# Seven products of half-size blocks in place of eight, in sixteen of 22 units of each up phase, with the inner tensor kept whole

## The reference, cut to what matters

```
def swiglu_ffn(x, w_in, w_out):              # twice: "up0/down0", "up1/down1"
    gate, up = jnp.split(x @ w_in, 2, axis=-1)
    return (jax.nn.silu(gate) * up) @ w_out
...
def conv_ffn(x, w_up, conv_w, conv_b, w_down):   # twice: "up2/down2", "up3/down3"
    up = x @ w_up
    a, g = up[..., :D_FF_2], up[..., D_FF_2:]
    g = causal_dwconv(g, conv_w) + conv_b        # three taps along the tokens
    return (jax.nn.gelu(g) * a) @ w_down
```

## Time and profile before

| | us |
|---|---|
| median of 3 runs | 2401.2 (2400.77 to 2401.31) |
| the profiled execution | 2402.46 |
| its span from first to last instruction | 2400.6 |
| TensorE busy | 2385.5 |
| VectorE busy | 1094.6 |
| ScalarE busy | 806.7 |
| GpSimd busy | 65.3 |
| mean granted TensorE clock | 0.998 of 2.4 GHz |

### The profile page before, as it was taken

One profiled execution on the slowest core, in us unless ns is written; L12 is line 12 of the kernel. 1 busy time (PEld: TensorE's weight loads), 2 busy tenths in 40 slices (PEclk: granted clock), 3 DMA queues, 4 the chain that ended last, 5 costly groups with the idle time before them and its releaser, 6 DMA issues.

```text
span 2400.6 us, 27033 instructions
## 1 busy us (share of the span) xinstructions
PE 2385.5 (99%) x12158; PEld 2026.4 (84%) x12158; DVE 1094.6 (46%) x1040; ACT 806.7 (34%) x891; POOL 65.3 (3%) x39
## 2 busy tenths in 40 slices
PE   9999999999999999999999999999999999999998
PEld 8888889898788888898987888888888977888887
DVE  4333225574553332256735544424545546544424
ACT  4222225455542222233432433322322432333311
POOL 0000000230100000000000000000000000000000
PEclk9999999999999999999999999999999999999999
DMA  4223323212132223142521222231432511222321
GB/s 163 103 91 105 106 88 126 76 37 88 39 120 90 104 90 112 70 164 87 177 73 56 103 101 95 98 115 66 153 106 72 191 70 71 88 105 88 122 90 68
DMA packets 34691, 238.30 MB, mean 99 GB/s; under 512 B 4108, under 2 KB 4492, under 8 KB 6800
## 3 DMA queue, kind: packets, MB, share of 16 engines
q1 hardware_dynamic: 34432, 236.56, 27.7%
q10 hardware_dynamic: 144, 0.00, 0.0%
HBM read 234.46 MB, written 2.10 MB: 99 GB/s over the span
## 4 chain that ended last, share of the span: by engine, by line
PE 98%; DVE 1%; ACT 1%; issue 0%; DMA 0%; DVEq 0%
PE bank L452 55%; PE bank L526 28%; PE bank L491 4%; PE bank L873 4%; PE bank L514 1%; PE bank L900 1%; PE bank L727 1%; PE bank L920 1%; PE bank L659 0%; PE bank L669 0%; PE bank L567 0%; DVE xn L1545 0%; PE bank L628 0%; PE bank L911 0%; PE bank L654 0%
## 5 line engine op out<-in xcount | busy, mean ns | idle before, releaser
L452 PE MATMUL bank<-a_hi,w_hi 128*128 128x512 f32 (+1 forms) x2112 | 787.2, 373 | 0.4 <-DVE a_lo L1590 0.4
L452 PE MATMUL bank<-a_hi,w_lo 128*128 128x512 f32 (+1 forms) x2112 | 782.8, 371 | 0.0
L452 PE MATMUL bank<-a_lo,w_hi 128*128 128x512 f32 (+1 forms) x2112 | 782.8, 371 | 0.0
L1520 DVE TENSOR_TENSOR w_lo<-raw,w_hi 128x2048 fp32r<-128x2048 f32 x207 | 476.5, 2302 | 502.3 <-ACT w_hi L1043 501.8
L1043 ACT ACTIVATE w_hi<-raw 128x2048 fp32r<-128x2048 f32 x207 | 394.5, 1906 | 357.2 <-DMA raw<-w_full 357.2
L452 PEld LDWEIGHTS bank<-a_hi,w_hi 128*128 128x128 f32 x2112 | 398.8, 189 | 69.9 <-issue 1.7
L452 PEld LDWEIGHTS bank<-a_hi,w_lo 128*128 128x128 f32 x2112 | 398.7, 189 | 67.7 <-issue 0.7
L452 PEld LDWEIGHTS bank<-a_lo,w_hi 128*128 128x128 f32 x2112 | 398.6, 189 | 67.1
L526 PE MATMUL bank<-w_hi,h_hi 128*128 128x512 f32 x692 | 270.1, 390 | 0.0
L526 PE MATMUL bank<-w_hi,h_lo 128*128 128x512 f32 x692 | 269.6, 390 | 0.0
L526 PE MATMUL bank<-w_lo,h_hi 128*128 128x512 f32 x692 | 269.6, 390 | 0.0
(11 more groups left out here) (297 smaller groups left out, 2320.1 us busy)
## 6 DMA issues: line engine op xcount, KB each, us to landing
raw<-w_full SPq DMA_DIRECT2D x207, 1024.0 KB, 4.8
rows_ab<-rows SPq DMA_DIRECT2D x8, 1024.0 KB, 5.4
x<-x SPq DMA_DIRECT2D x4, 512.0 KB, 6.4
mem_raw<-mem SPq DMA_DIRECT2D x2, 1024.0 KB, 8.2
out<-x SPq DMA_DIRECT2D x3, 512.0 KB, 2.6
raw<-w_full SPq DMA_DIRECT2D x2, 512.0 KB, 6.3
ab_rows<-ab_rows SPq DMA_DIRECT2D x1, 768.0 KB, 7.6
wg_raw<-w_gates SPq DMA_DIRECT2D x1, 512.0 KB, 5.8
```

The costliest lines, as they stand in the source:

```text
L452: last = mm(bank[:, b + m, cols], w[:, s, c0:c0 + P], act_in[:, k, cols], start=(k == 0 and j == 0), stop=(k == KD - 1 and j == 2))
L1520: V.tensor_tensor(w_lo[:, u % SLOTS, :], raw[:, u % SLOTS, :], w_hi[:, u % SLOTS, :], ALU.subtract).then_inc(w_split, 1)
```

## The change

Units 4 to 19 of each up phase (`SEVEN0`, `SEVEN1`), 64 in all, are computed as a 2x2 by 2x2 block product with seven products (the form with shared sums): the two row blocks are the gate's 128 columns and the other half's 128 columns of the unit, the inner dimension is halved to 4 tiles, and the tokens are halved to 256.

- **TensorE** (`seven_unit`): 7 products of 12 matmuls of 256 columns, into four banks, in place of 48 of 512 columns. Two products use `a_hi`/`a_lo` and the weights as they are; the others use sums of weights (`s23`, `s4`, and one in place in `raw`), sums of tokens (`t`), or both.
- **GpSimd** (`up`): at the start of an up phase, behind the split of the last tokens, four sums of token blocks, ten operations of 128x1024. For each of the 16 units four sums of 128x512: one in place in `raw` before ScalarE's copy, and three behind the sixth product of unit u - 2.
- **ScalarE**: high parts of the sums (128x1024 and 128x512 per unit), a copy of the first product out of PSUM, on which the unit's last product waits. The high part of the inner tensor moves to the down phase.
- **VectorE** (`seven_results`): five additions from PSUM that recombine the products into `gate_c` and `h32`; the taps and the multiply then read SBUF on both inputs. Low parts of the sums. The low part of the inner tensor moves to the down phase.
- The inner tensor is kept whole as `h32` (44 KB per partition) and split in four stages of two blocks (`hidden_high`, `hidden_low`) in the last two units of the up phase and in the down phase. The down phase takes tokens in order 0 to 3.
- Some semaphores are merged (`small_in`), and the gain rows are loaded behind unit 19 of the up phase.

The core of the diff:

```
+SEVEN0, SEVEN1 = 4, 20
...
+            def add_up(dst, terms):
+                (first, _), (second, op) = terms[:2]
+                ins = G.tensor_tensor(dst, first, second, op)
+                for term, op in terms[2:]:
+                    link(ins)
+                    ins = G.tensor_tensor(dst, dst, term, op)
+                return ins
...
+            def first_weight_sum(f, u):
+                g = U0[f"up{f}"] + u
+                w = raw[:, g % SLOTS, :]
+                gp.wait_ge(w_loaded[g % SLOTS], 16 * (g // SLOTS + 1))
+                G.tensor_tensor(w[:, 2 * QS:3 * QS], w[:, 2 * QS:3 * QS], w[:, 3 * QS:4 * QS],
+                                ALU.add).then_inc(first_sum, 1)
...
+                gp.wait_ge(first_sum, j + 1)
+                if u >= SEVEN0 + 2:
+                    gp.wait_ge(gemm_done, gemm_at(f"up{f}", u - 2, 0))
+                link(G.tensor_tensor(s2, w[:, 2 * QS:3 * QS], w[:, 0:QS], ALU.subtract))
+                G.tensor_tensor(s3, w[:, 3 * QS:4 * QS], s2, ALU.subtract)
+                G.tensor_tensor(s4, w[:, QS:2 * QS], s2, ALU.subtract).then_inc(rest_sums, 1)
+
+            def up(f):
+                gp.wait_ge(a_lo_tok, TURN0[UP_GEN[f]] + NT)
+                token_sums(f, 1)
+                token_sums(f, 3)
+                first_weight_sum(f, SEVEN0)
+                rest_weight_sums(f, SEVEN0)
+                token_sums(f, 2)
+                token_sums(f, 4)
+                first_weight_sum(f, SEVEN0 + 1)
...
+                pe.wait_ge(w_split, U0[name] + u + 1)
+                bank_wait(name, u)
+                product(b, 0, w, 0, b_block(0, 0)).then_inc(first_product, 1)
+                product(b + 1, 0, w, QS, b_block(1, 0))
+                pe.wait_ge(t_split, 4 * f + 2)
+                product(b + 2, 1, w, 2 * QS, t_block(1))
+                pe.wait_ge(s_split, j + 1)
+                product(b + 2, 0, s23, QS, t_block(3))
+                product(b + 3, 1, s4, 0, b_block(1, 1))
+                pe.wait_ge(t_split, 4 * f + 4)
+                product(b + 1, 1, s23, 0, t_block(2)).then_inc(gemm_done, 1)
+                pe.wait_ge(first_copied, j + 1)
+                product(b, 1, w, 3 * QS, t_block(4)).then_inc(gemm_done, 1)
...
+            def copy_first(f, u):
+                act.wait_ge(first_product, nth_seven(f, u) + 1)
+                S.activation(h32[:, u, 0:256], bank[:, up_bank(u), 0:256], ACT.Copy).then_inc(first_copied, 1)
+
+            def hidden_high(f, u):
+                act.wait_ge(*hidden_at(f, 2 * u + 1))
+                act.wait_ge(*stage_free(f, u))
+                S.activation(h_hi[:, stage(u), :], h32[:, 2 * u:2 * u + 2, :], ACT.Copy).then_inc(h_high, 1)
...
+            def low_sums(f, u):
+                j = nth_seven(f, u)
+                dve.wait_ge(s_high, j + 1)
+                V.tensor_tensor(s23_lo[:, j % 2, :], s23_raw[:, j % 2, :], s23_hi[:, j % 2, :], ALU.subtract)
+                V.tensor_tensor(s4_lo[:, j % 2, :], s4_raw[:, j % 2, :], s4_hi[:, j % 2, :],
+                                ALU.subtract).then_inc(s_split, 1)
...
+                    if is_seven(n + 2) and n + 2 > SEVEN0:
+                        split_upto(U0[name] + n + 2)
                     dve.wait_ge(gate_done, F0[f] + n + 1)
-                    dve.wait_ge(gemm_done, gemm_at(name, n))
-                    V.tensor_tensor(h32[:, s, :], act_out[:, s, :], bank[:, b + 1, :], ALU.mult).then_inc(ffn_banks, 1)
-                    dve.wait_ge(h_hi_done, F0[f] + n + 1)
-                    V.tensor_tensor(h_lo[:, n, :], h32[:, s, :], h_hi[:, n, :], ALU.subtract).then_inc(h_done, 1)
-                    split_upto(U0[name] + n + 3)
+                    if is_seven(n):
+                        dve.wait_ge(ffn_banks, F0[f] + n + 1)
+                        V.tensor_tensor(h32[:, n, :], gate_s[:, s, :], h32[:, n, :], ALU.mult).then_inc(h_done, 1)
```

More of the change, by code:

```diff
@@ new lines, in up @@
+            def up(f):
[7 more added lines that the diff above has]
+                first_weight_sum(f, SEVEN0 + 1)
+                for u in range(SEVEN0 + 1, SEVEN1):
+                    rest_weight_sums(f, u)
+                    if u + 1 < SEVEN1:
+                        first_weight_sum(f, u + 1)
@@ L461, in feature_units, with seven_unit, product, b_block @@
                         feature_tile(name, u, m, slice(0, T)).then_inc(gemm_done, 1)
+            def seven_unit(f, u):
+                name = f"up{f}"
+                j, s, b = nth_seven(f, u), (U0[name] + u) % SLOTS, up_bank(u)
+                w, acts = (w_hi[:, s, :], w_lo[:, s, :]), (a_hi, a_lo)
+                s23 = s23_hi[:, j % 2, :], s23_lo[:, j % 2, :]
+                s4 = s4_hi[:, j % 2, :], s4_lo[:, j % 2, :]
+                def product(dst, half, weights, c0, moving):
+                    (hi, lo), (m_high, m_low) = weights, moving
+                    for k in range(KD // 2):
+                        for i, (st, mv) in enumerate(((hi, m_high), (lo, m_high), (hi, m_low))):
+                            last = mm(bank[:, dst, 256 * half:256 * half + 256], st[:, c0 + k * P:c0 + k * P + P], mv[:, k, :],
+                                      start=(k == 0 and i == 0), stop=(k == KD // 2 - 1 and i == 2))
+                    return last
+                def b_block(k, n):
+                    return block_b(a_hi, k, n), block_b(a_lo, k, n)
+                def t_block(n):
+                    return t_hi[:, n - 1, :, :], t_lo[:, n - 1, :, :]
+                pe.wait_ge(w_split, U0[name] + u + 1)
[11 more added lines that the diff above has]
+                product(b, 1, w, 3 * QS, t_block(4)).then_inc(gemm_done, 1)
@@ L1001, in _ @@
             head_units("up0", "start")
-            feature_units("up0", 2, KF)
+            up_units(0)
             down("down0", 0)
@@ L1005, in _ @@
             head_units("up1", "mixout")
-            feature_units("up1", 2, KF)
+            up_units(1)
             down("down1", 1)
@@ new lines, in up, with down_parts @@
+                    if is_seven(n + 1):
+                        copy_first(f, n + 1)
+                    if n + 3 < SEVEN0:
+                        split_upto(U0[name] + n + 3)
+                    elif n + 2 >= SEVEN1:
+                        split_upto(U0[name] + n + 2 + max(0, min(n - SEVEN1 + 1, 1)))
+                    if n >= SEVEN1:
+                        hidden_high(f, n - SEVEN1)
+            def down_parts(f):
+                name = f"down{f}"
+                for u in range(KF - SEVEN1, UNITS[name]):
+                    hidden_high(f, u)
+                    split_upto(U0[name] + u + 1)
@@ L1615, in rms_out, with down_parts @@
+                    if n >= SEVEN1:
+                        hidden_low(f, n - SEVEN1)
+            def down_parts(f):
+                name = f"down{f}"
+                for u in range(KF - SEVEN1, UNITS[name]):
+                    hidden_low(f, u)
+                    split_upto(U0[name] + u + 1)
             def rms_out(name, again):
                 end = U0[name] + UNITS[name]
-                split_upto(end)
+                down_parts(int(name[-1]))
                 rows_ready(name)
```

256 lines of the change are left out of this document (206 added, 50 removed).

## The result

The changed kernel takes 2420.89 us in the median of 4 runs (2418.86 to 2422.9), the kernel before 2400.98 beside it (2400.54 to 2401.31): a ratio of 1.0083, 95% interval 1.0066 to 1.01. It is slower by 20 us; the forecast was 2421. The profiled execution took 2421.81 us.

The account below looks back on a forecast made before the run. TensorE, 98% of the chain, was taken as the bound before; VectorE and GpSimd turns bind convolution units after. Silu phases +18.8 and convolution phases -39.0 make 20 us slower: 2421 us, range 2371 to 2446.

Parts of the forecast that it names:

- TensorE's unit: Seven-product units on TensorE: 84 matmuls of 256 columns take 9.95 us (9.7 to 10.1) instead of 10.88.
- Turns: GpSimd sums and VectorE two-SBUF operations alternate, 1.15 us per sum; a convolution unit's turn is 12.0 us.
- A: Rival: sums and subtractions overlap without turns, VectorE's 8.6 us fit under 9.95; 2342 us, chance 0.06.
- B: Rival: in up2 and up3 sums fall beside PSUM additions more often, 10.2 us a unit; 2371 us, chance 0.18.
- Silu phases: up0 and up1: VectorE's 9.6 us stays under TensorE's 9.95; 14.9 gained less 5.5 at the start, each.
- Part 3: VectorE and GpSimd together in seven-product units: they take turns; 12.0 us with convolution, 9.6 with silu.
- rival C: up0 and up1: sums alternate as with the convolution, turn 10.5 us; 2438 us, chance 0.17 together with the clock rival D.
- Convolution phases: up2 and up3: 1.9 us gained, 15.6 lost to turns and 5.8 at the start, together -39.0 for both.
- Start: Unit 4 of each up phase waits for token sums at its sixth product; 5.5 us silu, 5.8 convolution (3 to 8).
- rival D: TensorE's clock falls after the stalls at unit 4, a few us more; chance 0.17 together with rival C.
- Hidden work: Inner-tensor split in the down phase, ScalarE copies and weight loads stay covered; without cover the splitting costs 2.2 us a unit.

Follow-up runs that it names:

- e4: Changed kernel, but GpSimd's three later weight sums of a unit also wait for VectorE's low parts of the unit before; all work done: 2390.11 us.
- e5: Changed kernel with token sums cut to their first operations, 4 of 128x1024 per up phase in place of 10: 2388.4 us.
- e1: Changed kernel with seven products only in up0 and up1, eight kept in up2 and up3: 2382.4 us, ratio 0.9921 to the kernel before.

## Why the prediction was right, step by step

- **TensorE's unit.** Predicted 9.95 us; 1260 matmuls in 149.44 us are 15 units of 9.96. Taking 0.118 for products without a twin held: the mean is 0.1186.
- **Turns.** Predicted 12.0 us with three held operations of 1.15; measured 12.11 (additions begin at 1425.54, 1437.65, 1449.75). The step that carried the forecast, read from two places of a few us in the trace of before, held in units 6 to 18. Rivals A and B fell with it: held operations are there, and the packing of B doesn't happen by itself. It can be had by ordering, and e4 goes part of the way, at 10.87 with two turns on the taps, where B had 10.2.
- **Silu phases.** Predicted +9.4 each, measured +8.0 and +10.0. The unit's work on VectorE, summed to 9.6, took 9.73, with the one held `w_lo` that Part 3 has. The margin was 0.2 us and it was enough: no unit from 6 on waits, so rival C fell. The difference between the two phases lies in their starts.
- **Convolution phases.** Predicted -19.5 each, measured -19.6 and -19.4. That it came out to 0.1 us was luck: the turns cost 16.7 us in up2 (13 units at 12.1 and unit 19 at 11.4) where the sum had 15.6, and the start 4.7 where it had 5.8.
- **Start.** Predicted a stall of 5.5 to 5.8 us. Unit 4 takes 16.4 us in up0 instead of 9.96 (61.99 to 78.42), 6.5 more, 14.8 in up1, 4.8 more, and 14.6 in up2 (1347.33 to 1361.88), 4.6 more. The size was about right, the place only in part. The prediction had the stall at the sixth product, behind the token sums' low part; its chain of 42 to 44 us against 40.4 gives 2 to 4 us there, and it took the upper end. That wait is 1.36 us in up2. The others stand before the fourth product, for the weight sums' low part (0.39 us in up2, 2.30 in up0), and before the last, for the copy (1.88 in up2); in up0 and up1 TensorE also waits 0.5 us before unit 5, for the multiply that frees its banks. A further assumption was too simple. I treated start and turns as costs that add up. With the start removed in e5 a convolution phase came out 11.0 us shorter, since a late VectorE needs five units to reach TensorE when it begins in time. For the changed kernel the sum was right only because its start had taken that lead away; for variants it misled me twice.
- **Clock, rival D.** Of the four starts the clock fell in that of up0 alone, and it cost nothing. Windows of up0 (busy time of PE, granted clock, DMA share and GB/s) with the first matmul behind the stall, first the changed kernel, then e1, which has the same start there:

```profile
68.70:71.00 2.30, 2.26 (x10) 0.50 0.00 0
68.74 0.58 PE L621 MATMUL bank<-t_hi,s_hi 128*128 128x256 f32 x1 [2.30 <-DVE s_lo L1839]
...
68.05:71.00 2.95, 2.92 (x24) 1.00 0.00 0
68.08 0.38 PE L630 MATMUL bank<-t_hi,s_hi 128*128 128x256 f32 x1 [2.30 <-DVE s_lo L1848]
72.55 0.38 PE L630 MATMUL bank<-t_hi,s_hi 128*128 128x256 f32 x1 [1.37 <-DVE t_lo L1856]
```

  Behind 2.30 us without work TensorE is granted 0.50, the 1.2 GHz level, in the changed kernel, and 14 matmuls start 0.21 us apart instead of 0.119, 1.3 us in all. In e1 the same wait is followed by a clock of 1.00. Its matmuls get on faster and then wait 1.37 us for `t_lo`, a wait that the changed kernel doesn't have in up0. Unit 4 takes 16.43 us with the fall and 16.46 without. In up2 the waits of 1.36 and 1.88 us were followed by a clock of 1.00.
- **Hidden work.** The split of the inner tensor cost nothing: between 254 and 355 us, in down0, TensorE is busy for 101.0 of 101.0 us, VectorE for 35.2 and ScalarE for 30.5. The down phase has the same 106.1 us as before.

What stays open is why the runs of the changed kernel spread over 4 us. Those of before spread over 0.8 in the four beside it, but over 2.8 in the fourteen beside the later runs (2400.08 to 2402.92). The stretch of the mixer that is 1.6 us longer in the traces with a clock of 0.98 there can be part of the answer, but of the four runs only the profiled one has a trace, so this is not shown.

## What to carry over

A shared resource is priced from the few places where two engines meet in the trace of before, by who ends how far behind whom; multiply by how often the new order makes them meet, not by busy time. Where two such queues must share, put the one's work beside what the other does out of PSUM, or thin the work until a pair of units has room: less saved on TensorE was worth more. And a cycle that is too long costs only from the unit in which the lead of the slow engine is used up, so a cost at the start and a cost per unit don't add.

## What the runs showed of the hardware

- GpSimd's sum of two 128x1024 operands in SBUF takes 2.40 us alone, 1.30 for 128x512. One of 128x512 that takes turns with VectorE ends 1.15 to 1.18 us behind VectorE's end, at each of the turns read above.
- A wait costs TensorE more than the idle time that the trace shows: waits of some 0.94 and 0.68 us in a unit made it 2.15 us longer, some 0.26 us more for each. A matmul of 256 columns is recorded with 0.28 us while they start 0.119 apart, so 0.16 of overlap is lost at each wait, and the first matmul behind one is recorded with 0.38, 0.1 more than its like.
- The clock after a wait differs between runs of the same work: behind 2.30 us without matmuls in up0 it was 0.50 in the changed kernel and 1.00 in e1. In e4, where the last product of unit 4 waits 2.6 to 3.1 us in each of the four phases, it was 0.50 behind each of these waits, at its end in three phases and 1.1 us later in up0.
